# Starting the arena of an on-chip memory layout at a multiple of 512 bytes

## The chip, the core and the metric

The kernel runs on one core of one Trainium2 chip. The core has a matrix engine (TensorE, PE in the profile), VectorE (DVE), ScalarE (ACT), GpSimd (POOL) and SyncE (SP), which here only issues transfers. On-chip memory has 128 partitions; an address below is a byte offset in a partition, the same in all 128. The metric is the device time of one execution in microseconds, the median of the runs shown.

## The reference, cut to what matters

Two transformer blocks are computed, one after the other, on one sequence of 512 tokens and 1024 features, in float32. The first block has a modulated RMS norm, native sparse attention (compressed, selected and window branches), an indexed sparse attention, an output projection and a feed-forward layer of width 4096 with a squared ReLU. The second has a SwiGLU layer, stick-breaking attention beside an RWKV-7 recurrence, an output projection, and a second SwiGLU layer:

```python
def swiglu(x, w_gate, w_up, w_down):
    return (jax.nn.silu(x @ w_gate) * (x @ w_up)) @ w_down

    x = x + FFN_HALF * swiglu(rms_norm_2(x, norm_ffn1[l]), ffn1_gate[l], ffn1_up[l], ffn1_down[l])
    ...
    x = x + jnp.concatenate([o_sb, o_rw], axis=-1) @ w_out[l]
    x = x + FFN_HALF * swiglu(rms_norm_2(x, norm_ffn2[l]), ffn2_gate[l], ffn2_up[l], ffn2_down[l])
```

## The kernel before

**How a large product is made.** Activations lie with features on partitions and the 512 tokens along the partition. A weight tile is loaded into one of four slots of `ring`; ScalarE rounds it to a high part, VectorE subtracts for a low part, and both go to one of three slots of `wsp`. Activations are split into high and low parts in the same way. One product of 128 features by 512 tokens is then three matmuls in float32r, at lines 363 (high weight, high activation), 364 (high weight, low activation) and 365 (low weight, high activation):

```python
                pe.matmul(out, lhs[0], rhs[0], start=start, stop=False)
                pe.matmul(out, lhs[0], rhs[1], start=False, stop=False)
                return pe.matmul(out, lhs[1], rhs[0], start=False, stop=stop)
```

The weights `lhs` stay in the array and the 512 columns of `rhs` stream through it; in the profile's names, `bank<-hids,wsp` streams `hids` against weights from `wsp`. Two token products are the other way round: their weights are slices of `hs`, and rows of `wsp` stream through (`bank<-wsp,hs`): `w_v` with rows of 348 columns, and `w_v2` with rows of 512.

**Where the streamed rows lie.** `hs` holds the split activations before a product. Four more tensors hold split activations in the arena, a region of 75,776 bytes that the stages of the program use in turn:

- `hids`, the hidden activations of the feed-forward layers: input of `w_down`, `down1` and `down2`.
- `h2a`, features 0 to 511 of the input of the second SwiGLU layer (`gate2`, `up2`); features 512 to 1023 lie in `hs`. A tile of 128 outputs is 12 matmuls from `h2a` and then 12 from `hs`.
- `orw`, the recurrence's output: half of the input of `w_out2`, 12 matmuls of a tile of 24.
- `oalt`, three of the eight parts of the input of `w_out`: 9 matmuls of a tile of 24.

Each begins a whole number of 1024 bytes after the arena's start, and each of their rows is 512 four-byte numbers, 2048 bytes. The arena also holds float32 tensors: the first modulation weights (`ada`, which the DMA queue of SP writes there; two of the eight go to `hal`, another name for the bytes of `hs`), the scores and probabilities of the attentions, and the recurrence's chunks. Those are multiplied in plain float32.

**Where the tensors start.** Helper `at` hands out addresses one after the other from 16,896 on, and rounds a size up to a multiple of 64 bytes. 16,896 is 33 x 512. The sizes of `x` (16,384), `hs` (32,768), `ring` (22,528) and `wsp` (33,792) are multiples of 512, so that `hs` starts at 33,280 and `wsp` at 88,576, both multiples of 512. The constants `cst` take 9,280 bytes, the vectors `col` 896, `ext` 4,608 and `tmp` 12,288: `tmp` starts at 137,152 and the arena at 149,440, both 448 bytes past a multiple of 512. A slot of `wsp` is 5,632 bytes a part, 11 x 512.

The order of the work is written out by hand, engine by engine, with semaphores.

Of the kernel before, what the change touches and what calls it, by code (L numbers as in the profile page):

```python
# [136 lines left out]
def build(nc, xt, consts, cols, pos, ada, ada_late, mats, extra, out):  # L137
    ctx = ExitStack()
    with ctx:
# [10 lines left out]
        place = [SBUF_START]  # L150

        def at(name, shape, dt=F32, offset=None):

            size = 4 * int(np.prod(shape[1:]))
            if offset is None:
                offset = place[0]
                place[0] += (size + 63) // 64 * 64
            return nc.alloc_sbuf_tensor_at(name, shape, dt, offset=offset), offset
# [9 lines left out]
        col, _ = at("col", [P, NCOLS])  # L168
        ext, _ = at("ext", [P, 2 * T + 2 * DH])
        tmp, _ = at("tmp", [P, 6, T])  # L170
        arena, arena_at = at("arena", [P, 74 * 256])
        hids, _ = at("hids", [P, 2, NG, T], F32R, arena_at)
        mod, _ = at("mod", [P, 48])
# [2222 lines left out]
```

## Time and profile before

| | before |
|---|---|
| median of 3 runs | 1938.95 us (1936.39 to 1939.06) |
| the profiled execution's own time | 1930.27 us |
| its span, from the first to the last instruction | 1928.5 us |
| PE busy | 1834.7 us |
| DVE, ACT, POOL busy | 936.6, 697.7, 135.5 us |
| HBM read | 168.33 MB |

The profiled execution is one run apart from the three. Busy times are sums over one engine; matmuls overlap, and a matmul's end is modelled, so the distance from one matmul's start to the next one's says what a matmul costs in a row of them.

### The profile page before, as it was taken

Reading aid. Unit: us, or ns where it says so; the run is one execution under the profiler, and the core shown is the slowest. Engines: PE = TensorE matmul, PEld = TensorE weight load, DVE = VectorE, ACT = ScalarE, POOL = GpSimd, SP = SyncE. Lnnn points to the kernel's source line nnn. Section 1 sums busy time; section 2 is a strip of 40 time slices with the busy share of each in tenths; the row PEclk is TensorE's granted clock in tenths of the full one; section 3 lists DMA queues with packets and bytes.
Section 4 is the critical chain, followed back from the end, with each engine's and each line's share of the span. In section 5 each row is a group of like instructions: output and inputs, shape, how many; then the busy total and the mean of one; then the engine's idle time right before and its main releaser. Section 6 shows DMA issues by size and latency. Waiting matters only on the chain.

```text
span 1928.5 us, 27690 instructions
## 1 busy us (share of the span) xinstructions
PE 1834.7 (95%) x11652; PEld 1414.4 (73%) x11652; DVE 936.6 (49%) x1482; ACT 697.7 (36%) x1055; POOL 135.5 (7%) x109
## 2 busy tenths in 40 slices
PE   5999989989999998999999999899988899999999
PEld 2666655768888886788888877555778678888887
DVE  5277886363434344544244444445754644434442
ACT  4225557242323133332133334577311533312320
POOL 0023444200000002000000010000000110000000
PEclk8999999989999999999999999999999999999999
DMA  9662101212222222223223212111000222322231
GB/s 379 259 246 88 50 12 34 87 45 99 95 91 99 98 93 83 76 94 119 72 99 108 100 66 86 56 38 39 24 4 4 77 97 89 127 70 88 99 126 39
DMA packets 44476, 176.15 MB, mean 91 GB/s; under 512 B 5569, under 2 KB 5825, under 8 KB 41025
## 3 DMA queue, kind: packets, MB, share of 16 engines
q1 hardware_dynamic: 44352, 174.38, 25.5%
q8 instruction: 93, 1.52, 0.3%
q14 instruction: 31, 0.25, 0.0%
HBM read 168.33 MB, written 2.10 MB: 88 GB/s over the span
## 4 chain that ended last, share of the span: by engine, by line
PE 85%; DVE 7%; DMA 3%; ACT 3%; issue 2%; SPq 0%; DVEq 0%; ACTq 0%
PE bank L363 24%; PE bank L364 23%; PE bank L365 23%; PE bank L507 2%; DMA arena<-ada_late 1%; PE bank L523 1%; PE bank L539 1%; PE bank L714 1%; PE bank L855 1%; DMA arena<-ada 1%; PE bank L872 1%; PE bank L863 1%; DMA ring<-m_w_v 1%; ACT wsp L1086 1%; DVE arena L2051 1%
## 5 line engine op out<-in xcount | busy, mean ns | idle before, releaser
L1561 DVE TENSOR_TENSOR wsp<-ring,wsp 128x1024 fp32r<-128x1024 f32 (+2 forms) x244 | 312.9, 1284 | 445.5 <-ACT wsp L1086 445.4
L363 PE MATMUL bank<-hs,wsp 128*128 128x512 f32 x1160 | 472.1, 407 | 16.0 <-DVE hs L1828 5.3
L1086 ACT ACTIVATE wsp<-ring 128x1024 fp32r<-128x1024 f32 (+2 forms) x244 | 268.7, 1103 | 597.4 <-PE bank L365 590.2
L364 PE MATMUL bank<-hs,wsp 128*128 128x512 f32 x1160 | 454.6, 392 | 0.0
L365 PE MATMUL bank<-hs,wsp 128*128 128x512 f32 x1160 | 453.8, 391 | 0.0
L363 PEld LDWEIGHTS bank<-hs,wsp 128*128 128x128 f32 x1160 | 218.9, 189 | 87.4 <-issue 30.7
L364 PEld LDWEIGHTS bank<-hs,wsp 128*128 128x128 f32 x1160 | 219.3, 189 | 49.7 <-issue 6.0
L365 PEld LDWEIGHTS bank<-hs,wsp 128*128 128x128 f32 x1160 | 219.1, 189 | 47.2
L365 PE MATMUL bank<-hids,wsp 128*128 128x512 f32 x608 | 239.6, 394 | 0.0
L363 PE MATMUL bank<-hids,wsp 128*128 128x512 f32 x608 | 239.6, 394 | 0.0
L364 PE MATMUL bank<-hids,wsp 128*128 128x512 f32 x608 | 239.6, 394 | 0.0
L364 PEld LDWEIGHTS bank<-hids,wsp 128*128 128x128 f32 x608 | 113.7, 187 | 28.2
L363 PEld LDWEIGHTS bank<-hids,wsp 128*128 128x128 f32 x608 | 113.7, 187 | 28.1
L365 PEld LDWEIGHTS bank<-hids,wsp 128*128 128x128 f32 x608 | 113.7, 187 | 28.1
L2192 POOL TENSOR_TENSOR arena<-arena 128x512 f32<-128x512 f32 x24 | 41.2, 1718 | 1182.0 <-ACT arena L1098 1182.0
L1886 DVE SCALAR_TENSOR_TENSOR x<-bank,x 128x512 f32<-128x512 f32 x40 | 27.7, 692 | 151.4 <-PE bank L365 151.4
L1292 ACT ACTIVATE hids<-tmp 128x512 fp32r<-128x512 f32 x44 | 27.8, 633 | 118.3 <-DVE tmp L1876 118.3
L363 PE MATMUL bank<-h2a,wsp 128*128 128x512 f32 x176 | 69.8, 396 | 0.0
L364 PE MATMUL bank<-h2a,wsp 128*128 128x512 f32 x176 | 69.3, 394 | 0.0
L365 PE MATMUL bank<-h2a,wsp 128*128 128x512 f32 x176 | 69.3, 394 | 0.0
L1199 ACT ACTIVATE arena<-arena,smin 128x512 f32<-128x512 f32 (+3 forms) x96 | 53.0, 556 | 24.1 <-DVE smin L1730 23.9
L1289 ACT ACTIVATE tmp<-tmp 128x512 f32<-128x512 f32 x44 | 27.8, 632 | 85.2 <-DVE tmp L1870 85.2
(340 smaller groups left out, 2107.5 us busy)
## 6 DMA issues: line engine op xcount, KB each, us to landing
ring<-m_gate SPq DMA_DIRECT2D x44, 512.0 KB, 3.4
ring<-m_up SPq DMA_DIRECT2D x44, 512.0 KB, 3.4
ring<-m_down SPq DMA_DIRECT2D x32, 704.0 KB, 4.0
ring<-m_w_in SPq DMA_DIRECT2D x38, 512.0 KB, 3.5
arena<-ada_late SPq DMA_DIRECT2D x16, 1024.0 KB, 7.0
ring<-m_w_up SPq DMA_DIRECT2D x32, 512.0 KB, 3.4
ring<-m_w_down SPq DMA_DIRECT2D x32, 512.0 KB, 3.4
ring<-m_w_out SPq DMA_DIRECT2D x16, 512.0 KB, 3.6
```

Of the source, the lines that this page charges most:

```text
L363: pe.matmul(out, lhs[0], rhs[0], start=start, stop=False)
L364: pe.matmul(out, lhs[0], rhs[1], start=False, stop=False)
L365: return pe.matmul(out, lhs[1], rhs[0], start=False, stop=stop)
L507: pe.matmul(bank[:, b, 0:kv], proj[DH * e:DH * e + DH, (QN, QN, QD)[br] + i, t * P:(t + 1) * P], proj[DH * e:DH * e + DH, (KSL, KW, KDD)[b ...
L523: mm = pe.transpose(bank[:, b, (c + k) * P:(c + k + 1) * P], soft[p % 4][:, e, k * P:(k + 1) * P], const("ident"))
L1086: act.activation(wsp[:, s % SPLIT, 0, 0:size], ring[:, i % RING, 0:size], ACT.Copy)\
L1199: act.activation(soft[p % 4][:, e, 0:kv], soft[p % 4][:, e, 0:kv], ACT.Exp, scale=-1.0, bias=smin[:, n:n + 1], accum_out=ssum[:, n:n + 1]) ...
L1289: act.activation(ftmp[:, n % 2, :], ftmp[:, n % 2, :], ACT.Silu).then_inc(S("silu"), 1)
L1292: act.activation(hids[:, 0, n, :], ftmp[:, n % 2, :], ACT.Copy).then_inc(S("hid2_hi"), 1)
L1561: dve.tensor_tensor(wsp[:, s % SPLIT, 1, 0:size], ring[:, i % RING, 0:size], wsp[:, s % SPLIT, 0, 0:size].bitcast(F32), ALU.subtract).then ...
L1886: dve.scalar_tensor_tensor(out=x[:, nn, :], in0=bank[:, nn % 4, :], scalar=scale, in1=x[:, nn, :], op0=ALU.mult, op1=ALU.add).then_inc(S(" ...
L2192: pool.tensor_tensor(sq_at(tag, 0), sq_at(tag, 0), sq_at(tag, k), ALU.add).then_inc(S("sq_sum"), 1)
```

## The change

One line rounds the next free address up to a multiple of 512 before the arena is placed:

```diff
         ext, _ = at("ext", [P, 2 * T + 2 * DH])
         tmp, _ = at("tmp", [P, 6, T])
+        place[0] = (place[0] + 511) // 512 * 512
         arena, arena_at = at("arena", [P, 74 * 256])
         hids, _ = at("hids", [P, 2, NG, T], F32R, arena_at)
```

The arena moves by 64 bytes, from 149,440 to 149,504, which is 292 x 512. `hids`, `oalt`, `orw` and `h2a` are placed from `arena_at` and move with it, and so do all views of the arena and the small tensors behind it (gains, gates, sums). `x`, `hs`, `ring`, `wsp`, `cst`, `col`, `ext` and `tmp` stay. No instruction is added, taken away or moved on any engine; only addresses differ, and every source line behind the new one has a number one higher.

## Rows read from the trace of the kernel before

**Rows 1.** The page: busy time of PE, and the chain that ended last.
```profile
PE 1834.7 (95%) x11652; PEld 1414.4 (73%) x11652; DVE 936.6 (49%) x1482; ACT 697.7 (36%) x1055; POOL 135.5 (7%) x109
...
PE 85%; DVE 7%; DMA 3%; ACT 3%; issue 2%; SPq 0%; DVEq 0%; ACTq 0%
```

**Rows 2.** Two windows: busy us per engine, granted clock, DMA share, GB/s.
```profile
900.00:950.00 50.00, 50.00 (x216) 40.04 (x216) 14.73 (x15) 8.81 (x8) 0.00 (x0) 1.00 0.23 82
1000.00:1050.00 50.00, 50.00 (x223) 41.39 (x222) 23.35 (x28) 15.25 (x19) 0.00 (x0) 1.00 0.30 102
```

**Rows 3.** Timeline of PE, streaming `hs`: start us, us, instruction.
```profile
1005.30 0.39 PE L365 MATMUL bank<-hs,wsp 128*128 128x512 f32 x1
...
1008.70 0.39 PE L365 MATMUL bank<-hs,wsp 128*128 128x512 f32 x1
```

**Rows 4.** Timeline of PE, streaming `hids`.
```profile
904.73 0.39 PE L363 MATMUL bank<-hids,wsp 128*128 128x512 f32 x1
...
911.73 0.39 PE L363 MATMUL bank<-hids,wsp 128*128 128x512 f32 x1
```

**Rows 5.** Groups by form: count, busy us and mean ns, idle before.
```profile
L363 PE MATMUL bank<-hids,wsp 128*128 128x512 f32 x608 | 239.6, 394 | 0.0
...
L363 PE MATMUL bank<-h2a,wsp 128*128 128x512 f32 x176 | 69.8, 396 | 0.0
...
L363 PE MATMUL bank<-orw,wsp 128*128 128x512 f32 x32 | 12.9, 404 | 5.0 <-DVE orw L2163 5.0
...
L363 PE MATMUL bank<-oalt,wsp 128*128 128x512 f32 x24 | 9.6, 398 | 1.4 <-DVE hs L1752 1.4
```

**Rows 6.** Timeline of PE, one tile of the second SwiGLU's gate or up product.
```profile
1652.42 0.39 PE L363 MATMUL bank<-h2a,wsp 128*128 128x512 f32 x1
...
1655.22 0.39 PE L363 MATMUL bank<-hs,wsp 128*128 128x512 f32 x1
...
1657.96 0.39 PE L363 MATMUL bank<-h2a,wsp 128*128 128x512 f32 x1
```

**Rows 7.** Timeline of PE, product `w_v2`: rows of `wsp` stream.
```profile
1204.68 0.39 PE L363 MATMUL bank<-wsp,hs 128*128 128x512 f32 x1
...
1209.44 0.39 PE L363 MATMUL bank<-wsp,hs 128*128 128x512 f32 x1
```

**Rows 8.** Timeline of PE, second tile of `w_v`: where its streamed row changes.
```profile
51.05 0.32 PE L364 MATMUL bank<-wsp,hs 128*128 128x348 f32 x1
...
52.80 0.32 PE L363 MATMUL bank<-wsp,hs 128*128 128x348 f32 x1
...
54.68 0.32 PE L363 MATMUL bank<-wsp,hs 128*128 128x348 f32 x1
...
56.57 0.32 PE L363 MATMUL bank<-wsp,hs 128*128 128x348 f32 x1
...
58.33 0.32 PE L365 MATMUL bank<-wsp,hs 128*128 128x348 f32 x1
```

**Rows 9.** Single lines on DVE and ACT: count, min/median/max ns, first and last start.
```profile
L1636 DVE TENSOR_TENSOR hs<-tmp,hs x8: 691/692/693, 39.1 to 47.4; 128x512 fp32r<-128x512 f32 x8
...
L1879 DVE TENSOR_TENSOR hids<-tmp,hids x44: 692/693/695, 797.6 to 1869.0; 128x512 fp32r<-128x512 f32 x44
...
L1098 ACT ACTIVATE arena<-x x40: 613/617/632, 11.7 to 1558.4; 128x512 f32<-128x512 f32 x40
L1098 ACT ACTIVATE arena<-arena x16: 612/616/620, 343.2 to 759.2; 128x512 f32<-128x512 f32 x16
```

**Rows 10.** Timeline of PE, plain float32 products that stream the arena.
```profile
1499.58 3.60 PE L1043 MATMUL bank<-arena,ext 128*128 128x512 f32 x8
1503.02 1.45 PE L1048 MATMUL bank<-arena,cst 128*128 128x512 f32 x3
```

**Rows 11.** Two windows, columns as in Rows 2: `ada` lands in `arena`, in `hal`.
```profile
12.00:20.00 8.00, 5.75 (x16) 2.09 (x17) 5.39 (x10) 3.93 (x8) 0.00 (x0) 1.00 1.02 429
28.00:33.00 5.00, 2.04 (x12) 0.16 (x8) 4.49 (x6) 1.36 (x1) 0.00 (x0) 0.78 1.01 426
```

## The prediction

> **What bounds the kernel now.** I began with the page. PE is busy for 1834.7 of 1928.5 us, and 85% of the chain that ended last is PE; DVE has 7% of it, DMA 3%, ACT 3% [rows 1]. So a saving on PE that lies in a stretch without gaps goes to the end undiminished, and a saving anywhere else mostly does not. The windows show what such a stretch looks like: in 50 us of `down1` and in 50 us of the first SwiGLU's next gate and up products PE is busy for all 50 us, at a granted clock of 1.00 (the level of 2.4 GHz), while DVE works 14.73 and 23.35 us, ACT 8.81 and 15.25 us, and the DMA engines 23% and 30% [rows 2]. The other engines have two thirds of their time left at best and half of it at worst.
>
> The next thing to read is the count in these windows: 216 matmuls in one, 223 in the other [rows 2], both of 512 columns, both against weights from `wsp`, neither with a gap. The timelines give the exact spacing. Streaming `hs`, 15 steps from start to start take 1008.70 - 1005.30 = 3.40 us, 226.7 ns each [rows 3]. Streaming `hids`, 30 steps take 911.73 - 904.73 = 7.00 us, 233.3 ns each [rows 4]. The 512 columns alone would take 213.3 ns at 2.4 GHz, so that there are 13.3 ns on top with `hs` and 20.0 ns with `hids`. The difference is 6.67 ns, or 16 columns, and 16 four-byte columns are 64 bytes, which is just what `hids` lacks to a multiple of 512.
>
> **Is it the start address?** What differs between the two groups is the streamed operand alone: `hs` starts at a multiple of 512 and `hids` 448 bytes past one. The other streamed tensors fall on the same two sides. Within a tile of the second SwiGLU, the 12 matmuls of `h2a` (448 past) take 1655.22 - 1652.42 = 2.80 us, 233.3 ns each, and the 12 of `hs` behind them 1657.96 - 1655.22 = 2.74 us [rows 6]. In `w_v2` rows of `wsp`, all at multiples of 512, stream at (1209.44 - 1204.68) / 21 = 226.7 ns [rows 7]. Some of these lie at a multiple of 2048, others 512 past one (88,576 is 43 x 2048 + 512, and the low part begins 5,632 later, at 46 x 2048), so that nothing above 512 seems to matter; the arena's new start is 73 x 2048. The product `w_v` shows more directly that a start within 512 bytes counts. Its rows have 1392 bytes, and its four streamed rows begin 0, 368, 224 and 80 bytes past a multiple of 512 in the same slot; their spacing is 1.75/11 = 159.1, 1.88/12 = 156.7, 1.89/12 = 157.5 and 1.76/11 = 160.0 ns [rows 8]. That is 3.3 ns between neighbours a few hundred bytes apart, where the columns are the same in number. What exactly is read twice or waits there, no row tells.
>
> **The change, part by part.** After it, `hids`, `h2a`, `orw` and `oalt` start as `hs` does, and I take their spacing to be 226.7 ns.
> - `hids`: 608 at each of lines 363, 364 and 365, 1824 matmuls with no idle time before them [rows 5]. 1824 x 6.67 ns = 12.16 us.
> - `h2a`: 176 a line, 528 in all [rows 5], in 44 tiles of 12 `h2a` and 12 `hs`. A tile takes 5.54 us [rows 6]; 24 x 226.7 ns = 5.44 us. The 0.10 us is 0.08 us of `h2a` and 0.02 us of the `hs` matmuls behind the switch, 2.74 instead of 2.72 us. 44 x 0.10 = 4.40 us.
> - `orw` and `oalt`: 32 and 24 a line [rows 5], 168 in all, 1.12 us. Each of their 16 tiles, and four places where `hs` follows `hids`, has a switch as above: 20 x 0.02 = 0.40 us.
>
> The sum over these 1824 + 528 + 168 = 2520 matmuls is 12.16 + 4.40 + 1.12 + 0.40 = 18.1 us.
>
> The rest I cost at nothing. The matmuls are covered by nothing, so no cover is lost; the weight splits that feed them have the slack of [rows 2], and streaming `hs` already runs at the faster spacing with them. DVE does not notice starts: a subtraction that reads `tmp` (448 past) and `hs` (0) takes 692 ns, one that reads `tmp` and `hids` (both 448 past) 693 ns, so `hids` at 0 beside `tmp` at 448 stays at 692 [rows 9]. ACT squares into the arena in 617 ns from `x` (0) and 616 ns from the arena (448) [rows 9]. Plain float32 products of the arena are spaced (1503.02 - 1499.58) / 8 = 0.430 us, two passes of 215 ns [rows 10]: with 1.7 ns a pass above the columns there is nothing to win, 8 to 15 matmuls a stage apart. The DMA engines move 429 GB/s while `ada` lands in the arena, and 426 while it lands in `hal`, at a multiple of 512 [rows 11], so the start of the program, where DMA is the bound, stays.
>
> Two bounds are left. If the 0.02 us behind a switch stays, the gain is (44 + 20) x 0.02 = 1.3 us less. If it also vanishes where plain float32 matmuls of the arena interrupt the streaming of `hs`, in 16 tiles of `w_in` and 14 of `w_in2` with up to five interruptions each, 30 x 5 x 0.02 = 3.0 us come on top. I take neither, the first because the loss follows a change of start and the starts become equal, the second because those matmuls differ in shape and passes too.
>
> The sum is made against the profiled execution: 1930.27 - 18.1 = 1912.2 us for its own time, a span of 1910.4. The median of the runs shown is 8.7 us above that execution; the same saving gives 1938.95 - 18.1 = 1920.9 us, which is my prediction. What a measurement of this kernel can tell from no change is about 0.2%, 3.9 us.
>
> **The rivals.**
> - *No effect: the region counts, not the start.* All four arena tensors lie above 149,000 bytes, `hs` and `wsp` below 122,368, so a slower region would give the same two spacings, and after 64 bytes it would still be the slower region: 1939 us. For it speaks that no float32r row of this program starts at a multiple of 512 up there. Against it speak the exact 64 bytes and the four neighbours of `w_v` [rows 8]. The Trainium skill would side with it: "SBUF — State Buffer", section "Door 1: The DMA port swizzle (why `[64,N]` ≈ `[32,N]`)", knows lines of 16 bytes and a penalty for each new line, and both starts are multiples of 16. By that rule the two spacings would not differ at all, so the trace disagrees with it here. Likewise "TensorE: Matmul & The Clock Gate", section "Back-to-back issue gap", has N/2.4 + 2.5 ns whatever the address, an estimate of 215.8 ns; no float32r row here is that fast.
> - *Half of it.* Only part of the 6.67 ns is the start, say the 3.3 ns between the rows of `w_v` [rows 8]: 2520 x 3.3 = 8.3 us, 1930.6 us. Against it: each of the 512-column groups has one of two spacings, none lies between.
> - *Slower.* The weights of `wsp` start at a multiple of 512 as well, and are loaded while the row streams. If the arena's rows, in step with them, lose what the row at 80 bytes loses against the one at 368, 3.3 ns more instead of less, 2520 matmuls cost 8.3 us: 1947.3 us. It decides from a spacing above 233.3 ns. Against it: `hs` is in step with `wsp` already, and it is the fast one [rows 3].
>
> **How the numbers follow.** 0.76 for the forecast, 0.02 for a gain beyond its bounds, 0.06 for half, 0.11 for no effect, 0.05 for slower. Faster by over 0.2% are the first three, 0.84; within 0.2% is no effect, 0.11; slower 0.05. The forecast's own range goes from 1920.9 - 3.0 - 1.4 = 1916.5 to 1920.9 + 1.3 + 1.4 = 1923.6, with 1.4 us for half the spread of the three runs. With half the gain in it the range is 1916 to 1931, and leaves out 0.16 of rivals and a few hundredths of the forecast's tails.
>
> **What would show it.** Right: 30 steps of `hids` in 6.80 us instead of 7.00, a tile of `gate2` in 5.44 us with its halves at 2.72 and 2.72, `hs` elsewhere still at 226.7 ns, about 220 matmuls or more in a gapless 50 us of `down1`, VectorE's lines 1636 and 1879 (1637 and 1880 then) still near 692 ns, and a span near 1910.4 us. The forecast is wrong if `hids` stays at 233.3 ns (region), lands between (half) or above (slower); or if the spacing falls as said but idle time appears in front of the first matmul of a product (line 364 then), waiting for `wsp`, which would mean that the splits do not keep up.

## The result and the profile after

The changed kernel takes 1916.88 us (median of 4 runs, 1915.48 to 1919.45) beside 1939.01 us before (4 runs, 1936.39 to 1945.91): a ratio of 0.9882, 95% interval 0.9854 to 0.9910. In a second measurement, below, it is 0.9905, interval 0.9888 to 0.9922. The forecast was 1920.9 us, a ratio of 0.9907.

The page after, busy time of the engines and the chain that ended last, stands beside [rows 1]:

```profile
PE 1826.2 (95%) x11652; PEld 1422.2 (74%) x11652; DVE 934.5 (49%) x1482; ACT 697.8 (36%) x1055; POOL 134.3 (7%) x109
...
PE 86%; DVE 7%; ACT 3%; DMA 2%; issue 2%; SPq 0%; DVEq 0%; ACTq 0%
```

The same two windows as in [rows 2], with the same columns (us of the window; busy us and count of PE, PEld, DVE, ACT, POOL; granted clock, DMA share, GB/s):

```profile
900.00:950.00 50.00, 50.00 (x222) 41.39 (x222) 16.56 (x16) 8.60 (x7) 0.00 (x0) 1.00 0.24 82
1000.00:1050.00 50.00, 50.00 (x222) 41.42 (x221) 23.32 (x28) 15.23 (x18) 0.00 (x0) 1.00 0.30 102
```

The counts were 216 and 223 and are now equal. The timeline of PE gives the spacing, first for `hids` (30 steps), then for a tile of the second SwiGLU, from its `hs` half to the next tile's `h2a` half and to the `hs` half behind it; lines have moved by one:

```profile
915.00 0.39 PE L365 MATMUL bank<-hids,wsp 128*128 128x512 f32 x1
...
921.80 0.39 PE L365 MATMUL bank<-hids,wsp 128*128 128x512 f32 x1
...
1645.10 0.39 PE L364 MATMUL bank<-hs,wsp 128*128 128x512 f32 x1
...
1647.82 0.39 PE L364 MATMUL bank<-h2a,wsp 128*128 128x512 f32 x1
...
1650.54 0.39 PE L364 MATMUL bank<-hs,wsp 128*128 128x512 f32 x1
```

30 steps of `hids` take 6.80 us, 226.7 ns each, where they took 7.00 us [rows 4]. The halves of a tile take 2.72 and 2.72 us, where they took 2.80 and 2.74 [rows 6].

The span, however, shrank by only 10.8 us in the two profiled executions, from 1928.5 to 1917.7. Where the rest went is read at a landmark, the first matmul that streams `oalt` (first and last start are the two numbers behind the durations), before, after, and in the second execution of the changed kernel:

```profile
L363 PE MATMUL bank<-oalt,wsp x24: 393/394/497, 336.3 to 376.4; 128*128 128x512 f32 x24
```
```profile
L364 PE MATMUL bank<-oalt,wsp x24: 389/389/498, 344.3 to 383.9; 128*128 128x512 f32 x24
```
```profile
L364 PE MATMUL bank<-oalt,wsp x24: 389/389/496, 351.2 to 390.8; 128*128 128x512 f32 x24
```

From there to the end the kernel before needs 1928.5 - 336.3 = 1592.2 us, the changed one 1917.7 - 344.3 = 1573.4 and, in its second execution with a span of 1925.8 us, 1574.6: 18.8 and 17.6 us less. All 2520 matmuls that gain lie in that part. Ahead of it the changed kernel took 8.0 and 14.9 us longer in these executions. That does not point to the change as the cause: in all eleven traces taken of other layouts than the one before, the landmark lies between 337.2 and 352.0 us, and at 343.0 us in a kernel of the experiments that leaves the arena 448 bytes past a multiple of 512, as it was. A window over the first 340 us shows what differs there (same columns; before, after, after again):

```profile
0.00:340.00 340.00, 296.66 (x1948) 194.08 (x1949) 218.73 (x593) 156.60 (x365) 94.29 (x85) 0.96 0.41 152
```
```profile
0.00:340.00 340.00, 299.56 (x1904) 195.27 (x1904) 216.19 (x592) 154.77 (x362) 92.98 (x85) 0.93 0.42 151
```
```profile
0.00:340.00 340.00, 298.65 (x1843) 195.93 (x1843) 212.78 (x574) 149.04 (x345) 88.22 (x81) 0.91 0.42 151
```

The granted clock is 0.96, 0.93 and 0.91: in this part, where PE still waits for transfers and for the attention's other engines, the clock goes to its lower level, 1.2 GHz, for a spell now and then, and how much of the time differs from execution to execution. From 60 to 80 us, for instance, it is 1.00 before and 0.83 in the changed kernel, from 175 to 200 us 1.00 and 0.86. Over whole executions the mean granted clock was 0.986 in the profiled one of before, and 0.978 to 0.983 in all 11 runs of before that were timed later, the fastest of which took 1933.88 us. So the profiled execution of before (1930.27 us) was a lucky one in this part, and its span is a poor measure of the change; the medians are not.

VectorE and ScalarE, for [rows 9], and the float32 products, for [rows 10], have not moved:

```profile
L1880 DVE TENSOR_TENSOR hids<-tmp,hids x44: 691/693/694, 799.7 to 1859.9; 128x512 fp32r<-128x512 f32 x44
```
```profile
L1099 ACT ACTIVATE arena<-x x40: 612/615/631, 11.7 to 1555.4; 128x512 f32<-128x512 f32 x40
L1099 ACT ACTIVATE arena<-arena x16: 611/612/617, 351.1 to 761.8; 128x512 f32<-128x512 f32 x16
```
```profile
1497.28 3.60 PE L1044 MATMUL bank<-arena,ext 128*128 128x512 f32 x8
1500.71 2.74 PE L1049 MATMUL bank<-arena,cst 128*128 128x512 f32 x6
```

The last pair gives (1500.71 - 1497.28) / 8 = 0.429 us a record, beside 0.430 before.

### The profile page after: what moved, and what is told of

It reads as the page before. It is cut to its first block, busy times and chain, and to the rows that moved or that the text cites. A ratio compares the mean times of both kernels' runs of the same rounds, so it can differ in the third digit from the quotient of the medians.

```text
span 1917.7 us, 27690 instructions
## 1 busy us (share of the span) xinstructions
PE 1826.2 (95%) x11652; PEld 1422.2 (74%) x11652; DVE 934.5 (49%) x1482; ACT 697.8 (36%) x1055; POOL 134.3 (7%) x109
## 4 chain that ended last, share of the span: by engine, by line
PE 86%; DVE 7%; ACT 3%; DMA 2%; issue 2%; SPq 0%; DVEq 0%; ACTq 0%
PE bank L364 24%; PE bank L365 23%; PE bank L366 23%; PE bank L508 2%; PE bank L524 1%; PE bank L540 1%; PE bank L715 1%; PE bank L856 1%; DMA arena<-ada 1%; PE bank L873 1%; PE bank L864 1%; DMA ring<-m_w_v 1%; PE bank L434 1%; DMA arena<-ada_late 1%; ACT wsp L1087 1%
## 5 line engine op out<-in xcount | busy, mean ns | idle before, releaser
L364 PE MATMUL bank<-hids,wsp 128*128 128x512 f32 x608 | 236.5, 389 | 0.0
L365 PE MATMUL bank<-hids,wsp 128*128 128x512 f32 x608 | 236.5, 389 | 0.0
L366 PE MATMUL bank<-hids,wsp 128*128 128x512 f32 x608 | 236.5, 389 | 0.0
```

## The experiments

Three theories stood against each other. *Start*: a streamed row that does not begin at a multiple of 512 is slow. *Region*: the high part of the partition is slow. *Relative start*: what counts is where the streamed row begins against where the weights begin, modulo some power of two; `hs` and `wsp` both began at multiples of 512, so that the trace of before cannot tell this from *start*. Below, a tensor's phase is its start modulo 512. Each of these kernels has lines like this in front of a tensor, and rounds up again behind it:

```diff
+        place[0] = (place[0] - 448 + 511) // 512 * 512 + 448
         hs, hs_at = at("hs", [P, 2, KD, T], F32R)
...
+        place[0] = (place[0] + 511) // 512 * 512
         ring, _ = at("ring", [P, RING, SLOT])
```

A kernel for which one time and no range is given was timed once. Single times of one kernel lie up to 13 us apart (the changed kernel's from 1914.70 to 1927.66), so that the spacings carry the argument and these times only go with it.

**`hs` at 448, arena at 0.**

> hs starts 448 bytes past a multiple of 512, the arena at a multiple (the two have changed places against the kernel before). If the start within 512 bytes sets the spacing: hids 226.7 ns, hs 233.3 ns, w_v2 (wsp streams) 226.7 ns. If the region of the partition sets it: hids was slow for lying high and stays at 233.3 ns, hs stays at 226.7 ns. If it is the start relative to that of the weights in wsp: as for the start.

Timeline of PE, streaming `hs` (30 steps) and `hids` (24 steps):

```profile
1010.06 0.39 PE L368 MATMUL bank<-hs,wsp 128*128 128x512 f32 x1
...
1017.06 0.39 PE L368 MATMUL bank<-hs,wsp 128*128 128x512 f32 x1
...
929.94 0.39 PE L367 MATMUL bank<-hids,wsp 128*128 128x512 f32 x1
...
935.38 0.39 PE L367 MATMUL bank<-hids,wsp 128*128 128x512 f32 x1
```

`hs` 233.3 ns, `hids` 226.7 ns. The two have changed places, although `hs` still lies low and `hids` high: *region* is out. The time was 1947.00 us, beside 1937.36 us for the kernel before; `hs` is streamed 3480 times (1160 a line), so that it is the dearer one to misplace. `w_v2` did not stay at 226.7 ns, as *start* has it for a row of `wsp` at 0; its spacing was 229.0 ns, the first sign that the weights (here `hs`, at 448) have a part in it.

**`wsp` at 448, `hs` and arena at 0.**

> Only the weights in wsp start 448 bytes past a multiple of 512; hs and the arena start at multiples. If the start of the streamed row alone counts: hs and hids 226.7 ns, and w_v2, where wsp streams, 233.3 ns. If the start relative to the weights counts: hs and hids leave 226.7 ns, and w_v2 is at 233.3 ns. If the region counts: all at 226.7 ns but hids at 233.3 ns.

Timeline of PE, `hs` (30 steps) and `w_v2` (21 steps):

```profile
1009.85 0.39 PE L366 MATMUL bank<-hs,wsp 128*128 128x512 f32 x1
...
1016.72 0.39 PE L366 MATMUL bank<-hs,wsp 128*128 128x512 f32 x1
...
1206.40 0.39 PE L365 MATMUL bank<-wsp,hs 128*128 128x512 f32 x1
...
1211.30 0.40 PE L365 MATMUL bank<-wsp,hs 128*128 128x512 f32 x1
```

`hs` is at 229.0 ns although its own start is unchanged, and `w_v2` at 233.3. *Start* alone is out; the time was 1929.19 us.

**All three at 448.**

> hs, wsp and the arena all start 448 bytes past a multiple of 512, so that streamed rows and weights are in step again. If the start of the streamed row counts: hs, hids and w_v2 all 233.3 ns, and some 20 us more than the changed kernel. If the start relative to the weights counts: all 226.7 ns, as in the changed kernel.

Timeline of PE, `hs` and `hids`, 30 steps each:

```profile
1010.03 0.39 PE L367 MATMUL bank<-hs,wsp 128*128 128x512 f32 x1
...
1016.83 0.39 PE L367 MATMUL bank<-hs,wsp 128*128 128x512 f32 x1
...
915.06 0.39 PE L368 MATMUL bank<-hids,wsp 128*128 128x512 f32 x1
...
921.86 0.39 PE L368 MATMUL bank<-hids,wsp 128*128 128x512 f32 x1
```

Both 226.7 ns with no operand at a multiple of 512, and 1919.94 us beside 1937.36. This is the decisive one: the arena has the phase that it had before, and the whole gain is there. From the landmark on, this kernel needs 1918.1 - 343.0 = 1575.1 us, like the changed one (1573.4 and 1574.6).

**Other phases.** Four kernels with `wsp` at 0 show what each relative start costs.

> hs starts 64, the arena 128 bytes past a multiple of 512; wsp at a multiple. If only a multiple of 512 is spared the cost: hs and hids both 233.3 ns. If the cost grows with the bytes that lack to the next multiple (64 bytes cost 16 columns): more than 233.3 ns. If a multiple of 64 or 128 is enough: hids at 226.7 ns. The rows of w_v, which start 0 to 368 bytes past, differ by only 3.3 ns, so values between 226.7 and 233.3 ns are likely too.

> Streamed rows start 192 (hs) and 256 bytes (hids) ahead of the weights modulo 512; in w_v2 wsp streams against weights in hs and so starts 192 bytes behind, that is 320 ahead. If the start relative to the weights sets the spacing: each gets a value of its own, above 226.7 ns as at 64 (229) and 128 (232), and w_v2 gets what hs gets at 320 in the next kernel. If it fell off again halfway, hids would be nearest to 226.7 ns.

> Streamed rows start 320 (hs) and 384 bytes (hids) ahead of the weights modulo 512; w_v2 starts 192 ahead. If the relative start sets the spacing: w_v2 here is spaced as hs in the kernel with hs at 192, hs here as w_v2 there, and 384 lies at or below the 233.3 ns of 448.

> Streamed rows start 32 bytes ahead of the weights (hs) and 32 behind (hids); w_v2 starts 32 behind as well. If the cost goes in whole steps of 64 bytes: hs 226.7 or 229 ns, hids and w_v2 226.7 or 233.3 ns. If it goes with every byte: about 228 ns and about 230 ns.

Timelines of PE, the first and the last of 30 steps: `hids` of the first kernel (phase 128), `hs` (192) and `hids` (256) of the second, `hs` (320) of the third, `hids` (480) of the fourth:

```profile
914.98 0.39 PE L366 MATMUL bank<-hids,wsp 128*128 128x512 f32 x1
...
921.95 0.40 PE L366 MATMUL bank<-hids,wsp 128*128 128x512 f32 x1
```
```profile
1010.04 0.39 PE L368 MATMUL bank<-hs,wsp 128*128 128x512 f32 x1
...
1017.04 0.39 PE L368 MATMUL bank<-hs,wsp 128*128 128x512 f32 x1
...
915.00 0.39 PE L366 MATMUL bank<-hids,wsp 128*128 128x512 f32 x1
...
921.80 0.39 PE L366 MATMUL bank<-hids,wsp 128*128 128x512 f32 x1
```
```profile
1009.90 0.39 PE L368 MATMUL bank<-hs,wsp 128*128 128x512 f32 x1
...
1016.76 0.39 PE L368 MATMUL bank<-hs,wsp 128*128 128x512 f32 x1
```
```profile
914.96 0.40 PE L368 MATMUL bank<-hids,wsp 128*128 128x512 f32 x1
...
921.96 0.40 PE L368 MATMUL bank<-hids,wsp 128*128 128x512 f32 x1
```

Spacings of 512-column float32r rows, read in the same way (20 to 30 steps, good to about 0.3 ns), by how far the streamed row begins ahead of the weights:

| bytes ahead, modulo 512 | streamed (kernel) | ns |
|---|---|---|
| 0 | `hs` (before), all (after), all (all three at 448) | 226.7 |
| 32 | `hs` (`hs` at 32) | 233.3 |
| 64 | `hs`, `hids` (`wsp` at 448), `hs` (`hs` at 64), `w_v2` (`hs` at 448) | 229.0, 229.0, 229.0, 229.0 |
| 128 | `hids` (arena at 128) | 232.3 |
| 192 | `hs` (`hs` at 192), `w_v2` (`hs` at 320) | 233.3, 233.3 |
| 256 | `hids` (arena at 256) | 226.7 |
| 320 | `hs` (`hs` at 320), `w_v2` (`hs` at 192) | 228.7, 229.0 |
| 384 | `hids` (arena at 384) | 232.0 |
| 448 | `hids` (before), `hs` (`hs` at 448), `w_v2` (`wsp` at 448), `w_v2` (`hs` at 64) | 233.3, 233.3, 233.3, 233.3 |
| 480 | `hids` (arena at 480), `w_v2` (`hs` at 32) | 233.3, 233.3 |

Where two kernels reach the same relative start by different tensors they agree, as at 192 and 320, where once `hs` streams against `wsp` and once `wsp` against `hs`. The pattern repeats after 256 bytes. 32 bytes cost as much as 192 or 448, so that it does not go by steps of 64 bytes, which the expectations had as one possibility, nor in proportion to the bytes. The values are means: taken in ns from the trace, every gapless step of `hids` is 226 or 227 ns at 0 and 233 or 234 at 448, but 225 to 232 at 64 and 228 to 241 at 128. The times were 1940.63 us (64 and 128), 1937.69 (192 and 256), 1950.01 (320 and 384) and 1958.72 (32 and 480). The last can be worked out: against the changed kernel, all of 2520 + 3480 matmuls are at 233.3 instead of 226.7 ns, 40 us more than 1919.38 is 1959.4. The same sum gives 1942, 1943 and 1940 for the other three; the third is 10 us off, in a run whose mean granted clock was 0.977, where the other three had 0.981 to 0.983.

**The changed kernel again, in five rounds.**

> The changed kernel once more, timed against the kernel before in five rounds. If the saving is the spacing of the 2520 matmuls and nothing else: 18.1 to 18.6 us less than before, a ratio of 0.9905. If the 22.1 us of the first measurement hold more than the spacing: a ratio near 0.988 again.

1919.38 us (6 runs, 1914.70 to 1927.66) beside 1936.99 (11 runs, 1933.88 to 1940.72), a ratio of 0.9905, interval 0.9888 to 0.9922. 17.6 us, as the spacing alone gives. This ratio lies inside the interval of the first measurement, which had four runs a side, so that its 22.1 us need no second cause.

**The arena at 256.**

```diff
+        place[0] = (place[0] - 256 + 511) // 512 * 512 + 256
         arena, arena_at = at("arena", [P, 74 * 256])
```

> The one line of the change with the arena 256 bytes past a multiple of 512 instead of at one; hs and wsp as before. If the start relative to the weights counts modulo 256: hids, h2a, orw and oalt at 226.7 ns, and the whole time as the changed kernel's, 0.9905 of before. If a multiple of 512 is needed in the whole program: no better than before.

Timeline of PE, `hids`, 30 steps:

```profile
915.00 0.39 PE L365 MATMUL bank<-hids,wsp 128*128 128x512 f32 x1
...
921.80 0.39 PE L365 MATMUL bank<-hids,wsp 128*128 128x512 f32 x1
```

226.7 ns, and 1921.41 us beside 1939.84 us: 0.9897, interval 0.9878 to 0.9916. A multiple of 256 does as well as one of 512. No phase of the table is better than 0 or 256, and the changed kernel has all its streamed 512-column rows there already, so that the runs point to no better version.

**Low weights 64 bytes off.** Which weights does the stream collide with, those in the array or those that are being loaded for the next matmul? The low part of each slot of `wsp` was put 64 bytes further on:

```diff
+LOW = SLOT + 16
+WPITCH = 2 * SLOT + 64
...
-        wsp, wsp_at = at("wsp", [P, SPLIT, 2, SLOT], F32R)
+        wsp, wsp_at = at("wsp", [P, SPLIT, WPITCH], F32R)
...
+        place[0] = (place[0] + 255) // 256 * 256
         arena, arena_at = at("arena", [P, 74 * 256])
```

> The low parts of the weights start 64 bytes past a multiple of 256, the high parts, hs and the arena at multiples. A matmul streams while the next one's weights are loaded. If the weights in use count: the matmul of the low weights is spaced 233.3 ns from the next (it starts 448 relative to them), the other two 226.7 ns. If the weights loaded meanwhile count: the matmul ahead of it (high weight, low activation) is the one with the long spacing, and the one of the low weights, behind which high weights are loaded, keeps 226.7 ns. Either way the mean lies between, near 229 ns. If the weights do not matter at all: 226.7 ns for all three.

Timeline of PE, `hids`; line 368 has the low weights:

```profile
914.63 0.39 PE L366 MATMUL bank<-hids,wsp 128*128 128x512 f32 x1
914.85 0.39 PE L367 MATMUL bank<-hids,wsp 128*128 128x512 f32 x1
915.08 0.40 PE L368 MATMUL bank<-hids,wsp 128*128 128x512 f32 x1
915.32 0.39 PE L366 MATMUL bank<-hids,wsp 128*128 128x512 f32 x1
...
917.40 0.39 PE L366 MATMUL bank<-hids,wsp 128*128 128x512 f32 x1
```

12 steps take 917.40 - 914.63 = 2.77 us, 231 ns each. Taken in ns from the trace over all of `hids`, the spacings from lines 366, 367 and 368 to the next matmul are 228.3, 229.1 and 235.9 ns. The longest is that from the low-weight matmul to the next, where the first of the two theories had it, and not that from the matmul ahead of it; but three matmuls take 693 ns, 13 ns more than 3 x 226.7 and not the one step of 6.7 that both gave, and the two others are longer as well. So the address of the weights matters part by part, neither theory gives the sizes, and which of the two loads it is stays open. The time was 1943.65 us beside 1939.84.

## Why the prediction was right, and where it was not

- *PE in gapless stretches sets the end.* Right. The chain is 86% PE, the windows are still full, and no new idle time stands in front of the products: 0.0 us for `hids` and `h2a`, 5.0 for `orw` and 1.4 for `oalt`, as in [rows 5]. The splits kept up.
- *226.7 ns for `hids`, `h2a`, `orw`, `oalt`.* Right in size: `hids` has 226.7 ns, and a tile 5.44 us with halves of 2.72. The bound of 1.3 us for a switch that stays is not needed, since the `hs` half fell from 2.74 to 2.72 us. The reason given for leaving that bound out, that the loss follows a change of start, is too wide: with the arena at 256 the starts still differ and both halves take 2.72 us, while with `hs` at 448 the loss moves to the `h2a` half, 2.74 us behind 2.80 of `hs`. The loss stands behind slow rows.
- *The sum of 18.1 us.* Shown by the part behind the landmark (18.8 and 17.6 us) and by the second ratio (17.6 us). The span of 1910.4 us that the prediction gave as a sign did not come, it was 1917.7: it was built on the one profiled execution of before, which was lucky ahead of the landmark. The further 3.0 us, where plain float32 matmuls interrupt `hs`, did not come. Behind such an interruption in `w_in2`, from the second matmul of `hs` on, seven steps take 1.61 us before and after, where 7 x 226.7 ns are 1.59 us:

```profile
1244.61 0.39 PE L364 MATMUL bank<-hs,wsp 128*128 128x512 f32 x1
...
1246.22 0.39 PE L365 MATMUL bank<-hs,wsp 128*128 128x512 f32 x1
```
```profile
1242.97 0.39 PE L365 MATMUL bank<-hs,wsp 128*128 128x512 f32 x1
...
1244.58 0.39 PE L366 MATMUL bank<-hs,wsp 128*128 128x512 f32 x1
```

- *Is it the start address?* This step failed, with no harm to the sum. It read "what differs between the two groups is the streamed operand alone" and took the streamed row's own start, modulo 512, for the cause. The runs show the start relative to the weights, modulo 256: with all three tensors at 448 everything runs at 226.7 ns, and with the weights alone at 448 everything leaves it. The sum held because the weights of 2520 matmuls lie in `wsp`, which starts at a multiple of 512, so that both readings give the arena the same place. The recorded prediction had no row that told the two apart, so that the right place came with some luck.
- *The four rows of `w_v`* [rows 8] were right as a sign against *region* and wrong as a sign for *start*: nothing in the table makes the row at 0 dearer than the one at 112 (368 modulo 256). Their spacing, too, goes with the relative start modulo 256. The row at 80 bytes, 160.0 ns in [rows 8], takes 1.76/11 = 160.0 ns again with all three tensors at 448, but 1.70/11 = 154.5 ns with `hs` at 448 and 1.69/11 = 153.6 ns with `hs` at 192, two kernels in which it begins 144 bytes ahead of the weights modulo 256:

```profile
58.03 0.32 PE L366 MATMUL bank<-wsp,hs 128*128 128x348 f32 x1
...
59.73 0.32 PE L368 MATMUL bank<-wsp,hs 128*128 128x348 f32 x1
```
```profile
56.69 0.32 PE L366 MATMUL bank<-wsp,hs 128*128 128x348 f32 x1
...
58.38 0.32 PE L368 MATMUL bank<-wsp,hs 128*128 128x348 f32 x1
```

  So for these rows the best offset is not 0. A row of 1392 bytes also ends elsewhere than it began, modulo 256, and no run here takes that apart.
- *No effect.* Out, by `hs` and `hids` changing places. The page "SBUF — State Buffer" of the Trainium skill, section "Door 1: The DMA port swizzle (why `[64,N]` ≈ `[32,N]`)", with its lines of 16 bytes, would have all phases of the table equal, since all are multiples of 16; the trace has 226.7 to 233.3 ns.
- *Half of it.* Out for this change, but its counterargument was wrong in general: spacings of 229 and 232 ns do exist, at 64 and 128 bytes.
- *Slower.* Its mechanism, rows and weights in step, is the opposite of what happens: in step is the fast case for rows of 512 columns.
- DVE, ACT and the float32 products at nothing: right, as the rows after show.

## What to carry to other kernels

When a run of float32r matmuls has no gaps, read their spacing from start to start and compare it between operands; here 6.7 ns of 233.3 hid behind a modelled duration. Place streamed rows of 512 columns and the weights that they meet at the same offset modulo 256 bytes, 0 or 448 alike: moving one tensor alone can cost as much as it can give, as `hs` at 448 shows (1947.00 us beside 1937.36). For rows of another length, try offsets; those of 348 columns were fastest at 144, of the offsets that occur here. A start rounded up to 64 bytes by an allocator is not enough, and whether a single profiled span shows such a gain depends on the clock in its early part, so use the medians and a landmark.

## What was not expected of the hardware

The spacing of streamed rows depends on where the weights lie as well: the same stream of 512 columns is spaced 226.7, 229, 232 or 233.3 ns on the mean by the 256-byte offset between the two, in steps that do not follow the offset in proportion (32 bytes cost 6.7 ns, 64 bytes 2.3). Plain float32 products, at 0.430 us a record before and 0.429 after the arena's move by 64 bytes, show nothing of it.
